# Second block: gates through Tanh with a product on VectorE, later copies on VectorE, steps in other slots

## What is computed

```python
h = rms_norm_2(x, pre_norm_g[l])
aq, ak, av, ag, bq, bk, bv, bg = split(h @ w_in[l])      # 512 x4, 512, 128, 128, 512 columns
# A: 4 heads, two score maps each (64 lanes), values of 128 columns
a  = softmax(q0 k0 + bias) - lam * softmax(q1 k1 + bias)
oa = rms_norm_2(a @ av, diff_subln_g[l]) * (1.0 - lam_init)
ya = oa * silu(ag)
# B: 8 query heads, 2 key/value heads, 64 columns
ob = softmax(rope(norm(bq)) rope(norm(bk))) @ bv
yb = ob * silu(bg)
y = concatenate([ya, yb]) @ w_out[l]
x = x + rms_norm_2(y, post_norm_g[l])
```

## Time and profile before

| | |
|---|---|
| median of three runs | 1162.9 us (1162.29 to 1163.93) |
| profiled execution | 1160.94 us, its span 1159.3 us, granted TensorE clock 0.931 |
| busy over the span | PE 1095.4 us (94%), DVE 767.2 (66%), ACT 557.3 (48%), POOL 92.1 (8%) |
| HBM read | 217.46 MB, 188 GB/s over the span |
| slots of layer 0 | about 884.2 to 972.2 us |
| slots of layer 1 | about 1051.0 to 1139.0 us |

### The profile page before, as it was taken

How to read it: one execution, slowest core, us unless ns; L and a number is a source line. 1 busy time by engine, 2 the same in 40 slices (tenths; PEclk the granted TensorE clock), 3 DMA queues, 4 the chain that set the end, 5 groups by cost and what they waited for, 6 DMA issues and landing times.

```text
span 1159.3 us, 18344 instructions
## 1 busy us (share of the span) xinstructions
PE 1095.4 (94%) x6096; PEld 942.7 (81%) x6096; DVE 767.2 (66%) x1364; ACT 557.3 (48%) x925; POOL 92.1 (8%) x146
## 2 busy tenths in 40 slices
PE   6998998999999999999999999999999879799886
PEld 6776786899899778889997899899788667688665
DVE  5687758778886677787867546545686543775633
ACT  1555653435534367544443445434555643554732
POOL 1111101000000100100000000000020100110200
PEclk8799888899999799999998999999999969799969
DMA  9875555587786468666774355653466110565201
GB/s 372 296 253 199 182 182 202 172 301 268 271 291 253 149 201 286 253 219 219 255 250 154 124 167 181 211 187 118 154 219 191 55 37 19 175 215 163 64 9 45
DMA packets 58071, 219.12 MB, mean 189 GB/s; under 512 B 6532, under 2 KB 12420, under 8 KB 51880
## 3 DMA queue, kind: packets, MB, share of 16 engines
q1 hardware_dynamic: 49232, 170.02, 43.0%
q0 software_dynamic: 5760, 41.95, 9.9%
q10 hardware_dynamic: 3032, 6.57, 1.8%
HBM read 217.46 MB, written 1.06 MB: 188 GB/s over the span
## 4 chain that ended last, share of the span: by engine, by line
PE 75%; issue 10%; DVE 7%; ACT 4%; POOL 2%; DMA 2%; DVEq 0%; ACTq 0%; SPq 0%; POOLq 0%
PE ps L1569 22%; PE ps L1570 22%; PE ps L1571 22%; DVE w_lo L930 2%; PE ps L1664 2%; PE ps L1654 1%; PE ps L1636 1%; PE ps L1618 1%; POOL rinv L437 1%; PE ps L1931 1%; ACT w_hi L530 1%; ACT ada_raw L660 1%; PE ps L1628 1%; DMA arena<-in_adastream 1%; ACT both L872 1%
## 5 line engine op out<-in xcount | busy, mean ns | idle before, releaser
L930 DVE TENSOR_TENSOR w_lo<-raw,w_hi 128x1024 fp32r<-128x1024 f32 (+1 forms) x318 | 358.5, 1169 | 58.9 <-ACT w_hi L530 52.9
L530 ACT ACTIVATE w_hi<-raw 128x1024 fp32r<-128x1024 f32 (+1 forms) x318 | 308.4, 1009 | 137.9 <-DMA raw<-in_wstream 95.0
L1569 PE MATMUL ps<-w_hi,h_hi 128*128 128x512 f32 (+1 forms) x480 | 195.7, 408 | 8.9 <-DVE h_lo L1019 5.8
L1569 PE MATMUL ps<-h_hi,w_hi 128*128 128x256 f32 x704 | 203.2, 289 | 0.6 <-DVE h_lo L1011 0.4
L1570 PE MATMUL ps<-h_lo,w_hi 128*128 128x256 f32 x704 | 201.4, 286 | 0.0
L1571 PE MATMUL ps<-h_hi,w_lo 128*128 128x256 f32 x704 | 201.4, 286 | 0.0
L1570 PE MATMUL ps<-w_lo,h_hi 128*128 128x512 f32 (+1 forms) x480 | 190.1, 396 | 0.0
L1571 PE MATMUL ps<-w_hi,h_lo 128*128 128x512 f32 (+1 forms) x480 | 189.9, 396 | 0.0
L1569 PEld LDWEIGHTS ps<-h_hi,w_hi 128*128 128x128 f32 x704 | 137.6, 195 | 3.7 <-issue 2.2
L1570 PEld LDWEIGHTS ps<-h_lo,w_hi 128*128 128x128 f32 x704 | 137.5, 195 | 0.7
L1569 PE MATMUL ps<-w_hi,a_hi 128*128 128x512 f32 x352 | 137.4, 390 | 0.7 <-DVE a_lo L1337 0.7
(11 more groups left out here) (187 smaller groups left out, 1369.3 us busy)
## 6 DMA issues: line engine op xcount, KB each, us to landing
raw<-in_wstream SPq DMA_DIRECT2D x296, 512.0 KB, 5.4
ada_raw<-in_adastream POOLq DMA_DIRECT2D x40, 1024.0 KB, 5.2
ada_raw<-in_adastream SPq DMA_DIRECT2D x4, 1024.0 KB, 9.1
arena<-in_adastream SPq DMA_DIRECT2D x4, 1024.0 KB, 10.7
raw<-in_wsmall SPq DMA_DIRECT2D x22, 128.0 KB, 2.1
row<-in_gate_rows ACTq DMA_DIRECT2D x5, 512.0 KB, 4.3
row<-in_params ACTq DMA_DIRECT2D x2, 769.0 KB, 4.2
x<-in_x SPq DMA_DIRECT2D x1, 1024.0 KB, 9.2
```

What stands on the lines that cost most here:

```text
L530: act.activation(w_hi[:, c % SPLIT, at], raw[:, n, 0:width // 2], ACT.Copy)\
L930: nc.vector.tensor_tensor(w_lo[:, c % SPLIT, at], raw[:, (2 * c + h) % RAW, 0:width // 2], w_hi[:, c % SPLIT, at].bitcast(F32), ALU.subtract)\
L1569: nc.tensor.matmul(dst, sh, mh, start=start, stop=False)
```

## The change

Gates: ScalarE writes tanh(z / 2) from the bank (`gate_tanh`, slots 4 and 8 instead of 4 and 9), and VectorE multiplies (tanh + 1) by the bank (slots 5 and 9), in place. The missing factor 0.5 goes into the sub-norm gain (GpSimd) for ag and into the copy of bv for bg. Copies of T into prob_T for n = 4 to 11 move to VectorE, behind the maximum of the slot. On TensorE the steps of chunk 15 move from slots 8 and 9 to 6 and 7; tp0 and tp1 go to banks 0 and 1 instead of 2 and 3; the output steps of chunks 16 and 17, each four k in slots 14 to 17, become half steps of two k in slots 11, 12, 14 to 18 and one behind the slots. The high part of chunk 19 moves from ScalarE's slots 10, 11 to 9, 10; `operand_lo(0)` moves from VectorE's slot 11 to 10.

```diff
--- before.py
+++ after.py
@@ -250,6 +250,7 @@
         s_norm = sem("head_normalised")
         s_qk2lo = sem("second_operand_lo_done")
         s_comb = sem("differences_done")
+        s_gtanh = sem("gate_tanh_done")
         s_scores_seen = sem("scores_seen")
         s_relb = sem("relb_loaded")
         s_row = sem("row_loaded")
@@ -495,7 +496,7 @@
                 pool.wait_ge(s_row, layer * 16 + 96)
                 pool.sem_inc(s_step, 1)
                 own.inc(nc.gpsimd.tensor_scalar(row[:, R_SUB:R_SUB + P], row[:, R_SUB:R_SUB + P],
-                                                row[:, R_OML:R_OML + 1], None, ALU.mult))
+                                                row[:, R_OML:R_OML + 1], 0.5, ALU.mult, ALU.mult))
                 own.wait()
                 for t in range(TT):
                     pool.wait_ge(s_cp, layer * 12 + (8 + t + 1))
@@ -818,7 +819,8 @@
                 lsplit(5, CW)
                 for t in range(TT):
                     ready(0, t)
-                    act.activation(bv[:, t, :], ps[:, t, P:2 * P], ACT.Copy).then_inc(s_cp, 1)
+                    act.activation(bv[:, t, :], ps[:, t, P:2 * P], ACT.Copy, scale=0.5)\
+                        .then_inc(s_cp, 1)
                     act.activation(sq_b[:, t, 0:P], ps[:, t, 0:P], ACT.Square).then_inc(s_qsq, 1)
                 for k in range(2):
                     lsplit(6 + k, CW)
@@ -849,16 +851,23 @@
                 lsplit(15, CW)
 
 
-                for i in range(18):
-                    if i in (3, 5, 7, 9) or i >= 10:
-
-                        n = (i - 3) // 2 if i < 10 else i - 6
+
+
+                def gate_tanh(j, dst, banks):
+
+                    for t in range(TT):
+                        ready(j, t)
+                        act.activation(dst[:, t, :], ps[:, banks[t], :], ACT.Tanh, scale=0.5)\
+                            .then_inc(s_gtanh, 1)
+
+                for i in range(17):
+                    if i in (3, 5, 7, 9):
+
+                        n = (i - 3) // 2
                         act.wait_ge(s_pT, layer * 12 + (16 + n + 1))
                         act.wait_ge(s_pv, layer * 12 + (16 + n))
-                        src = ps[:, 6, :]
-                        src = backward(src) if n < 4 else src.rearrange("p (a i) -> p a i", i=P)
-                        act.activation(prob_T.rearrange("p (a i) -> p a i", i=P), src, ACT.Copy)\
-                            .then_inc(s_pTc, 1)
+                        act.activation(prob_T.rearrange("p (a i) -> p a i", i=P),
+                                       backward(ps[:, 6, :]), ACT.Copy).then_inc(s_pTc, 1)
                     if i < 16:
                         act.wait_ge(s_max, layer * 16 + (16 + i + 1))
                         if i == 9:
@@ -884,21 +893,21 @@
                                                   accum_out=ss8[:, 0, 2 * hh + t:2 * hh + t + 1])
                         last.then_inc(s_yss, 1)
                     if i == 4:
-                        evict(5, sub_gate, ACT.Silu, (2, 3))
-                    if i == 9:
-                        evict(6, b_gate, ACT.Silu, (0, 1))
+                        gate_tanh(5, sub_gate, (2, 3))
+                    if i == 8:
+                        gate_tanh(6, b_gate, (0, 1))
                     if i in (2, 3):
                         hi_part(C_SECOND + 16, i - 2, CW, layer, C_LAYER)
                     if i in (5, 6):
                         hi_part(C_SECOND + 17, i - 5, CW, layer, C_LAYER)
                     if i in (7, 8):
                         hi_part(C_SECOND + 18, i - 7, CW, layer, C_LAYER)
-                    if i in (10, 11):
-                        hi_part(C_SECOND + 19, i - 10, CW, layer, C_LAYER)
+                    if i in (9, 10):
+                        hi_part(C_SECOND + 19, i - 9, CW, layer, C_LAYER)
                     if i == 10:
-                        operand_hi(0, 2, layer * 4 + (4 + 1))
+                        operand_hi(0, 0, layer * 4 + (4 + 1))
                     if i == 13:
-                        operand_hi(1, 3, layer * 4 + (4 + 2))
+                        operand_hi(1, 1, layer * 4 + (4 + 2))
                     if i == 16:
                         operand_hi(2, 4, layer * 4 + (4 + 3))
                 operand_hi(3, 5, layer * 4 + (4 + 4))
@@ -1468,6 +1477,20 @@
                         nc.vector.tensor_reduce(negmax[:, i % 3, :],
                                                 ps[:, 4 + i % 2, :].rearrange("p (a b) -> p a b", b=S),
                                                 AX_X, ALU.max, negate=True).then_inc(s_max, 1)
+                    if 10 <= i <= 17:
+
+                        n = i - 6
+                        dve.wait_ge(s_pT, layer * 12 + (16 + n + 1))
+                        dve.wait_ge(s_pv, layer * 12 + (16 + n))
+                        nc.vector.tensor_copy(prob_T, ps[:, 6, :]).then_inc(s_pTc, 1)
+                    if i in (5, 9):
+
+                        dst, banks, n = ((sub_gate, (2, 3), 0), (b_gate, (0, 1), 2))[i // 9]
+                        for t in range(TT):
+                            dve.wait_ge(s_gtanh, layer * 4 + (n + t + 1))
+                            nc.vector.scalar_tensor_tensor(
+                                dst[:, t, :], dst[:, t, :], 1.0, ps[:, banks[t], :], ALU.add,
+                                ALU.mult).then_inc(s_cp, 1)
                     if i in (4, 6, 8, 10):
 
                         hh = (i - 4) // 2
@@ -1529,12 +1552,12 @@
                         lo_part(C_SECOND + 18, 0, CW, layer, C_LAYER)
                     if i == 10:
                         lo_part(C_SECOND + 18, 1, CW, layer, C_LAYER)
-                    if i == 11:
-                        operand_lo(0, 2, layer * 4 + (4 + 1))
+                    if i == 10:
+                        operand_lo(0, 0, layer * 4 + (4 + 1))
                     if i in (12, 13):
                         lo_part(C_SECOND + 19, i - 12, CW, layer, C_LAYER)
                     if i == 13:
-                        operand_lo(1, 3, layer * 4 + (4 + 2))
+                        operand_lo(1, 1, layer * 4 + (4 + 2))
                     if i == 17:
                         operand_lo(2, 4, layer * 4 + (4 + 3))
                 operand_lo(3, 5, layer * 4 + (4 + 4))
@@ -2024,25 +2047,27 @@
                 for i in range(19):
                     if i < 4:
                         gate_step(12, (2, 3), i // 2, i % 2)
-                    if i in (4, 5):
+                    if 4 <= i < 8:
                         if i == 4:
                             pe.wait_ge(s_cp, layer * 12 + 8)
-                        gate_step(14, (0, 1), 0, i - 4)
-                    if i in (8, 9):
-                        gate_step(14, (0, 1), 1, i - 8)
+                        gate_step(14, (0, 1), (i - 4) // 2, i % 2)
                     if i == 10:
-                        pe.wait_ge(s_cp, layer * 12 + 10)
+                        pe.wait_ge(s_cp, layer * 12 + 12)
                         pe.wait_ge(s_ya, layer * 4 + 2)
-                        transpose_pair(2, tiles(y_a, 0, 1)).then_inc(s_oT, 1)
+                        transpose_pair(0, tiles(y_a, 0, 1)).then_inc(s_oT, 1)
+                    if i in (11, 12):
+                        pe.wait_ge(s_h, layer * 8 + (24 + 1))
+                        out_step(16, 0, i - 11, range(2))
                     if i == 13:
                         pe.wait_ge(s_ya, layer * 4 + 4)
-                        transpose_pair(3, tiles(y_a, 2, 3)).then_inc(s_oT, 1)
-                    if i == 14:
+                        transpose_pair(1, tiles(y_a, 2, 3)).then_inc(s_oT, 1)
+                    if i in (14, 15):
                         pe.wait_ge(s_h, layer * 8 + (24 + 2))
-                    if i == 16:
-                        pe.wait_ge(s_cp, layer * 12 + 12)
-                    if 14 <= i <= 17:
-                        out_step(16 + (i - 14) // 2, (i - 14) // 2, i % 2, range(4))
+                        out_step(17, 1, i - 14, range(2))
+                    if i in (16, 17):
+                        out_step(16, 0, i - 16, range(2, 4))
+                    if i == 18:
+                        out_step(17, 1, 0, range(2, 4))
 
                     if i in (4, 6, 8, 10) or i >= 11:
 
@@ -2103,6 +2128,7 @@
                         transpose_pair(4, tiles(y_b, 0, 1)).then_inc(s_oT, 1)
 
 
+                out_step(17, 1, 1, range(2, 4))
                 pe.wait_ge(s_h, layer * 8 + (24 + 3))
                 for cb in range(2):
                     out_step(18 + cb, cb, 0, range(4, 6))
```

## The result

The changed kernel takes 1169.4 us (median of five runs, 1166.0 to 1171.9) against 1162.9 us: ratio 1.0053, interval 1.003 to 1.0077. It is 6.5 us slower, clear of noise. Its profiled execution took 1166.95 us, with a span of 1165.3 us where the kernel before had 1159.3.

The account below looks back on a forecast made before the run. It took the slots to be bound by TensorE's gaps, from the chain between engines, and by its low clock. +5.4 us a layer, +10.8 on the profiled 1160.94, gave 1171.7; with 2.0 to the median 1173.7, range 1156 to 1181.

Parts of the forecast that it names:

- Steps 1 and 2: Gates: four table loads a layer go (5.1 us of ScalarE); products on VectorE 1.35 us a gate, slot 9's not hidden.
- Step 3: Eight copies (n = 4 to 11) on VectorE at 0.69 us each, net 0 to +0.2 us a slot.
- Step 4: Slots 6 to 10: T for n=2 at 917.6, n=3 1.9 us earlier, tp0 unchanged at 926.4, clock low from there.
- Steps 5 and 6: Slots 10 and 11: clock low; first half step waits 3.7 us for operand_lo, PV4 at 937.9 (before: 931.63).
- Step 7: Slot 12: half step starts at 942.1, clock taken back at about 943.3, tp1 waits for VectorE until 948.8.
- Steps 8 and 9: Slots 13 to 18: clock falls again, chunk 17's step at 956.1, chunks 18 and 19 at 977.6, +5.4 us a layer.
- Rival A: Clock high from slot 11 on: faster, -2.8 to -4.8 us a layer, 1157 to 1153 us; chance 0.25.
- Rival B: Clock back about 4.5 us into slot 11 and again after slot 14's: +1.0 us a layer, 1165; chance 0.16.
- Rival C: Clock not raised before slot 14 or 15: +7.6 to +10.4 us a layer, 1178 to 1184; chance 0.16.
- D: Tanh placed in a set without Exp: four loads stay, 1.3 to 2.6 us a layer more, 1177 to 1179; chance 0.05.

Follow-up runs that it names:

- e11_before_filled: The kernel before with its own TensorE gaps filled by unused matmuls of 512 columns; 1143.2 us, ratio 0.9845 to the kernel before.
- e1_gates: The kernel before with the gates alone changed (Tanh on ScalarE, products on VectorE in slots 5 and 10); 1161.2 us, ratio 0.9998.
- e2_copies: The kernel before with only the copies for n = 4 to 11 moved to VectorE; 1165.5 us, ratio 1.0032.
- e12: e10 with the copies for n = 4 to 11 on VectorE again; 1136.9 us, ratio 0.9766 to the kernel before.
- e10: e6_operands_first with the copies back on ScalarE and unused matmuls in three TensorE gaps; 1131.4 us, ratio 0.9745 to the kernel before.
- e5_filled: The changed kernel with unused matmuls of 512 columns ahead of five TensorE waits; 1147.2 us, ratio 0.9882 to the kernel before.
- e6_operands_first: The changed kernel with operand_hi and operand_lo of tp0 and tp1 ahead of the Exp and maximum of slots 10 and 13; 1148.6 us, ratio 0.9862.
- e3_steps: The kernel before with only the new places of steps, banks, operands and chunk 19; Silu gates and ScalarE copies kept; 1164.9 us, ratio 1.0031.

## Why the prediction was right, and where its terms were off

It forecast slower, 1173.7 us in 1156 to 1181, and 1169.4 was measured. The mechanism is the one that it named, with one addition: e11_before_filled shows that a high clock throughout would have helped the kernel before nearly as much. Times below are moved by the 1.49 us between the two T for n=1, unless they are called its own.

- Steps 1 and 2, the gates: right that the loads go, and that the product on VectorE holds up tp0. e1_gates shows the part's worth as nothing, 0.9998. The Trainium skill's rule that exp and tanh share a set (ScalarE: Activation LUTs, "Table sets: the hidden batching unit") holds here: no load is left in the slots. The 2.66 us for a switch in its section "What ACT_TABLE_LOAD costs" is not what the trace of before shows: the Silu starts 1.30 us after the start of its load (907.00 and 908.30, 928.71 and 930.01), with no more than 0.02 us idle ahead of the load.
- Step 3, the copies: a little too low. The price of one was taken at 0.69 and was 0.689. Its net cost was put at 0 to +0.2 us a slot; e2_copies shows 3.7 / 16 = 0.23 and the slot stretches of e12 and e10 show 4.5 / 16 = 0.28. What was missed is that before, ScalarE's copy and VectorE's maximum and y_b product ran side by side; on one engine they add up, and the product is what the next PV waits for.
- Step 4: T for n=2 at 917.6 forecast, 917.5 measured; T for n=3 924.0 and 923.8; tp0 926.4 and 926.1, behind the product as said.
- Steps 5 and 6: the wait in slot 11 was put at 3.7 us and was 3.54, the half step at 935.3 and 934.3. Two terms made that 1 us. The clock was taken as low for all of slot 10; by its own time it was low from 921.3 to about 928.1 and then high for part of the scores and for T4, which came at 930.1 instead of 930.7. And VectorE's queue was added up too long: the copy was put 1.0 us behind the maximum of slot 10 and took 0.6, since T4 was there in time.
- Step 7: the clock's return at 943.3 was the step most at risk; measured about 943.3 (941.8 in its own time). It was taken and not worked out, and inside slot 10 the clock did what was not forecast, so that it fits this well is in part luck. tp1 was put at 948.8 and came at 948.0.
- Steps 8 and 9: wait in slot 14 3.5 forecast and 3.17 measured; the half step at 956.1 and 954.7; chunks 18 and 19 at 977.6 and 976.3. So 4.1 us a layer instead of 5.4. The gap of 1.3 had opened by slot 14 (1.4 there) and stays.
- The sum: 2 x 5.4 = 10.8 forecast, 2 x 4.1 = 8.2 in the slots, and 6.0 in the span. The other 2.2 us lie outside the slots: 1.5 ahead of the first T named and 0.6 between the two slot stretches. Ahead of that T all kernels do nearly the same, yet it comes at 907.0 to 913.9 us in their profiles, and runs of the kernel before differ by 12 us among themselves (1155 to 1167 over all groups), so the 2.2 us are put down to that, without proof.
- Rival A (clock high from slot 11 on, faster) did not come by itself; e5_filled shows what it would have been worth, and it was priced well: with slot 10 fast as well it was put at -4.8 us a layer against the kernel before, and the slot stretch of e5_filled is 63.6 - 58.8 = 4.8 shorter. The rest of what took the time to 1147 instead of 1153 lies outside the slots (in the profiles 1.5 us ahead of them and 2.1 between them), and A's ratio of 0.992 lies within the interval of e5_filled (0.9831 to 0.9932). Rival B (the clock back 4.5 us into slot 11) did not happen: it came back 9 us behind the start of the half step (932.81 and 941.8 in its own time). Rival C (half steps too thinly spread to raise the clock) did not happen in the profiled run of the changed kernel, but the profile of e6_operands_first shows it in slots 13 to 16. D is excluded.

What stays open: why e3_steps is 3.6 us slower by its ratio and only 0.9 in the slots of its profile, and which part of that is waits and which is clock, since no experiment filled its gaps alone; and the copies' cost in the whole time, which the profiles of e10 and e12 show but their intervals don't.

## What to carry to other kernels

Before an instruction is put ahead of a chain that sets the pace, add up what its operand's producer has queued ahead of it; here 3.3 us of a maximum, copies, a product and a lo part (928.72 to 932.00) stood before 0.7 us of operand_lo, and moving that up, with operand_hi on ScalarE, took 1.9% off. Freeing one engine is worth nothing if the work lands in front of the step that the other engines wait for: in e1_gates 5.1 us of table loads a layer went, and PV4, which had waited 1.67 us for the copy behind them, waited 1.8 for the product. And compare versions at equal clock, for example with filled gaps, before judging an order of work: both kernels here had more to win by the clock than the change could win or lose.

## What the runs showed of the hardware

That TensorE is busy doesn't mean that its clock is high: in e6_operands_first it was busy for all of the 22 us from 942 to 964 at a granted clock of 0.50, its time going to half steps of 512 columns between PVs of 64 columns and scores on 64 lanes. Which of these keeps the clock low, no run tells. Unused matmuls of 512 columns on 128 lanes in the gaps, the one before tp1 among them, kept the clock at 1.00 through all slots in four kernels, and took 18 to 20 us off two that otherwise did the same. The time of one and the same program can hang on this: the runs of e6_operands_first lay at 1141 (mean clock 0.954) and 1157 (0.939). With filled gaps the spread shrank in e5_filled, to 1146.8 to 1149.2 in four runs, but not in e10_first_filled, whose six runs lay at 1126.6 to 1135.8.
